# Sixteen buffers for value pages in the residual's place, half of a norm moved into the SSM stage, an operand split in pieces, and the decode product with the cached V turned round

## What is computed

```python
def layer_step(x, lp, sb_fn, s0_re, s0_im, mem_k, mem_v):
    x = half_ffn(x, lp['g_ffn1'], lp['w_ffn1_gate'], lp['w_ffn1_up'], lp['w_ffn1_down'])
    proj = rmsnorm(x, lp['g_mix']) @ lp['w_in']                  # q, k, v, u
    o_sb = sb_fn(q, k, v, lp['sb_bias'])                         # samples: 8192 cached keys each
    o_ssm, s_re, s_im = s5_mix(u, s0_re, s0_im, ...)             # ends in g * sigmoid(g @ w_glu + b_glu)
    mixed = jnp.concatenate([rmsnorm(o_sb, lp['g_sb_out']), rmsnorm(o_ssm, lp['g_ssm_out'])], axis=-1)
    x = x + mixed @ lp['w_out']
    x = x + cross_attend(rmsnorm(x, lp['g_xattn']), lp['w_xq'], lp['w_xo'], mem_k, mem_v)
    x = half_ffn(x, lp['g_ffn2'], lp['w_ffn2_gate'], lp['w_ffn2_up'], lp['w_ffn2_down'])

def memory_kv(mem, g_mem, w_xk, w_xv):
    hm = rmsnorm(mem, g_mem)
    return hm @ w_xk, hm @ w_xv          # the prompt's 256 memory rows

def cross_attend(h, w_xq, w_xo, mem_k, mem_v):
    s = jnp.einsum('blhd,bmhd->bhlm', q, mem_k) * (X_HEAD_DIM ** -0.5)
    o = jnp.einsum('bhlm,bmhd->blhd', jax.nn.softmax(s, axis=-1), mem_v)
```

## Time and profile before

| | us |
|---|---|
| median of 3 runs | 3155.11 (3146.27 to 3157.51) |
| the profiled execution | 3153.33 |
| its span | 3151.7 |
| TensorE busy | 2832.8 (90% of the span) |
| VectorE busy | 1722.9 (55%) |
| ScalarE busy | 905.1 (29%) |
| GpSimd busy | 635.7 (20%) |
| mean granted clock | 0.931 |

### The profile page before, as it was taken

One profiled execution on the slowest core, in us unless ns is written; L12 is line 12 of the kernel. 1 busy time (PEld: TensorE's weight loads), 2 busy tenths in 40 slices (PEclk: granted clock), 3 DMA queues, 4 the chain that ended last, 5 costly groups with the idle time before them and its releaser, 6 DMA issues. The chain is left out here.

```text
span 3151.7 us, 45173 instructions
## 1 busy us (share of the span) xinstructions
PE 2832.8 (90%) x15561; PEld 2272.7 (72%) x15561; DVE 1722.9 (55%) x2217; ACT 905.1 (29%) x1691; POOL 635.7 (20%) x827
## 2 busy tenths in 40 slices
PE   6778899999999899988869679998989999999998
PEld 4456565665666677855514669877989999999997
DVE  7559999988989945247350353544253222222226
ACT  4221111121111123059600441422043233333324
POOL 1010123223223000000122050022002223332223
PEclk8788999999999999999878789997899999999999
DMA  9866799989989711100366231134101111111111
GB/s 357 328 208 190 260 313 338 318 313 316 319 311 348 225 41 54 40 28 28 110 213 216 60 121 47 41 114 163 51 29 53 47 43 44 40 40 53 41 46 54
DMA packets 337781, 469.77 MB, mean 149 GB/s; under 512 B 26422, under 2 KB 215219, under 8 KB 336028
## 3 DMA queue, kind: packets, MB, share of 16 engines
q1 hardware_dynamic: 299748, 341.35, 33.1%
q0 software_dynamic: 37296, 125.54, 11.3%
q10 hardware_dynamic: 552, 0.57, 0.1%
HBM read 448.99 MB, written 18.39 MB: 148 GB/s over the span
## 5 line engine op out<-in xcount | busy, mean ns | idle before, releaser
L83 DVE TENSOR_TENSOR wlo<-raw,whi 128x1024 fp32r<-128x1024 f32 (+1 forms) x182 | 221.6, 1227 | 399.3 <-ACT whi L79 399.3
L106 PE MATMUL banks<-ffn_ghi,whi 128*128 128x344 f32 (+1 forms) x880 | 323.5, 368 | 68.8 <-DVE ffn_glo L1612 37.5
L79 ACT ACTIVATE whi<-raw 128x1024 fp32r<-128x1024 f32 (+1 forms) x192 | 197.5, 1041 | 612.7 <-PE banks L108 477.0
L1823 POOL TENSOR_TENSOR xT<-xT,ffn_down 128x344 f32<-128x344 f32 x264 | 249.2, 946 | 550.6 <-ACT ffn_down L1867 546.5
L106 PE MATMUL banks<-ffn_hhi,whi 128*128 128x344 f32 x1056 | 340.0, 322 | 8.4 <-DVE ffn_hlo L136 5.7
L107 PE MATMUL banks<-ffn_hlo,whi 128*128 128x344 f32 x1056 | 338.8, 321 | 0.0
L108 PE MATMUL banks<-ffn_hhi,wlo 128*128 128x344 f32 x1056 | 338.8, 321 | 0.0
L606 POOL DMA_DIRECT2D ffn_vt<-in_cache_v_dram x384 | 206.1, 537 | 648.9 <-issue 635.2
L619 DVE TENSOR_TENSOR ffn_kt<-ffn_kt,ffn_q 128x1024 f32<-128x1024 f32 x256 | 311.6, 1217 | 39.1 <-DMA ffn_kt<-in_cache_k_dram 38.9
L108 PE MATMUL banks<-ffn_ghi,wlo 128*128 128x344 f32 (+1 forms) x880 | 315.7, 359 | 0.0
L624 DVE TENSOR_REDUCE ffn_z<-ffn_kt 128x16 f32<-128x1024 f32 x256 | 311.7, 1218 | 6.5
(11 more groups left out here) (427 smaller groups left out, 4993.9 us busy)
## 6 DMA issues: line engine op xcount, KB each, us to landing
ffn_kt<-in_cache_k_dram SPq DMA_DIRECT2D x512, 256.0 KB, 4.3
ffn_vt<-in_cache_v_dram POOLq DMA_DIRECT2D x384, 256.0 KB, 5.2
raw<-in_w_ffn_gate_dram SPq DMA_DIRECT2D x44, 512.0 KB, 3.9
raw<-in_w_ffn_up_dram SPq DMA_DIRECT2D x44, 512.0 KB, 4.0
raw<-in_w_ffn_down_dram SPq DMA_DIRECT2D x44, 512.0 KB, 4.6
s_vt<-in_cache_v_dram SPq DMA_DIRECT2D x64, 256.0 KB, 4.3
s_vt<-in_cache_v_dram POOLq DMA_DIRECT2D x64, 256.0 KB, 4.5
a_wide<-in_w_ffn_gate_dram SPq DMA_DIRECT2D x11, 1024.0 KB, 9.8
```

Of the source, the lines that this page charges most:

```text
L79: act.activation(self.k.whi[c % W_RING][:, 0:self.width], self.k.raw[:, c % RAW_RING, 0:self.width], ACT.Copy).then_inc(self.hi_done, 1)
L83: dve.tensor_tensor(self.k.wlo[c % W_RING][:, 0:self.width], self.k.raw[:, c % RAW_RING, 0:self.width], self.k.whi[c % W_RING][:, 0:self.w ...
L106: pe.matmul(out, whi, rhi, start=first, stop=False)
L1823: pool.tensor_tensor(x, x, dt_[:, m % DR, 0:n], ALU.add).then_inc(added, 1)
```

## The change

It has six parts.

1. `Values.VR` is 16, and `s_vt` lies where `xT` lies. `xT` is written to a scratch in DRAM at attention's start (`x_away`) and read back in the SSM stage's SyncE program once all pages are weighed (`x_back`). The first 16 pages are asked for early: eight by SyncE before ck, the taps and the pages' weights, eight by GpSimd before it makes its mask. Two waits on TensorE's progress before the page loop are gone.
2. The norm of oT's prompt columns (`first_half`) is made in the SSM stage: squares on ScalarE after the states, additions, inverse and products on VectorE, sums on TensorE after the second part of y, roots on ScalarE before the third take. ScalarE waits for the twelve products before the turn takes.
3. glu's operand is split in three pieces of 344 columns, and TensorE waits for one piece a tile. The high parts of glu's first weights are made between the takes.
4. In memory the rows are loaded ahead (`rows_ahead`), only ossm and the eight sample columns of oT are normed, and all of that is on ScalarE and VectorE; GpSimd has nothing. The weight ring there has four buffers.
5. In all stages with `Late`, the wlo of units 1 and 2 are VectorE's, placed between the operand's pieces.
6. In cross, weights padded to 32 columns (a sample's four at b, b + 8, b + 16, b + 24) are stationary and V moves, 512 columns at a time, 32 matmuls that all add into PSUM partitions 0 to 31 of two banks. A mask product on VectorE keeps each head's own columns, and 8 matmuls with `sel` sum and turn them. GpSimd makes pad and mask at the stage's start.

```diff
+    def __init__(self, k, name, width=D, more=()):
         self.k, self.width = k, width
+        self.slots = [k.raw[:, r] for r in range(RAW_RING)] + list(more)
+        self.ring = len(self.slots)
...
-    def pool_ahead(self, pool):
-
-        for n in (1, 2):
-            pool.wait_ge(self.w.lo_done, n + RAW_RING)
-            self.w.lo(pool, n, n)
...
         self.w.lo(v, 0, 0)
+        later = {self.late.count() - 4: 1, self.late.count() - 1: 2}
         for m in range(self.late.count()):
             self.late.lo(v, m)
+            if m in later:
+                self.w.lo(v, later[m], later[m])
...
-                if self.late and n == 0:
-                    v.wait_ge(self.w.lo_done, 3 + RAW_RING)
...
+                if self.operand and n == 0:
+                    self.operand(pe, t)
...
-    VR = 8
+    VR = 16
...
+    FIRST_PAGES = range(VR)
+    OTHERS = range(VR, COUNT * 64)
+
     def prepare(self, pool):
+        pool.wait_ge(self.pages_in, 16)
+        pool.wait_ge(self.k.x_away, 16)
+        self.load(pool, 0, self.FIRST_PAGES)
         pool.memset(self.mask[:, :], 1.0).then_inc(self.consts, 1)
...
+        for n in pages[parity::2]:
...
+                sp.dma_start(self.x_dram, self.xT[:, :, :].rearrange("p k n -> p (k n)")).then_inc(self.x_away, 16)
...
+        self.first_half = Late(self, "mn0", [(0, 344), (344, 344), (688, 336)], lambda k, t0, n: self.oT[:, k, t0:t0 + n], None, None,
+                               None, place("s_nsquare", [P, 4, 344], 26.5), place("s_nacc", [P, 3, 344], 16),
+                               place("s_nroot", [P, NT], 60), place("s_nmean", [P, 3, 344], 21.125), [4, 5], blocks=4)
+        self.m_rows = place("m_rows", [P, 2, D], 0)
+        late_v = Values(self, self.nc.alloc_sbuf_tensor_at("s_vt", [P, Values.VR, 512], F32, offset=self.x_offset), place("s_vw", [P, Values.COUNT, 512], 41.25),
...
+                sp.wait_ge(late_v.pages_in, 16)
+                sp.wait_ge(self.x_away, 16)
+                late_v.load(sp, 1, late_v.FIRST_PAGES)
                 for i in range(2):
...
-                sp.wait_ge(late_v.pages_in, 16)
-                sp.wait_ge(q["gm_in"], 32)
-                sp.wait_ge(q["quad"], kinds["final"])
-                late_v.load(sp, 1)
+                late_v.load(sp, 1, late_v.OTHERS)
...
+                sp.wait_ge(late_v.v_used, 16 * Values.COUNT)
+                sp.dma_start(self.xT[:, :, :].rearrange("p k n -> p (k n)"), self.x_dram).then_inc(self.x_back, 16)
+                sp.wait_ge(q["taken"], kinds["turn"] + 9)
+                sp.dma_start(self.m_rows[:, :, :], a["mem_prompt"].rearrange("(b p) n -> p b n", p=P)).then_inc(self.rows_ahead, 16)
...
-                pool.wait_ge(q["quad"], kinds["final"])
-                late_v.load(pool, 0)
+                late_v.load(pool, 0, late_v.OTHERS)
...
+                act.wait_ge(q["v"], self.ssm_states)
+                for t_ in range(3):
+                    self.first_half.squares(act, t_)
                 for i in range(8):
+                    if i == 2:
+                        for t_ in range(3):
+                            self.first_half.roots(act, t_)
...
+                act.wait_ge(q["scaled"], 12)
                 for i in range(8):
+                    if i == 6:
+                        for n in range(2):
+                            glu.w.hi(act, n, n, 1)
...
-                act.activation(ghi[:, :, :], gT[:, :, :], ACT.Copy).then_inc(q["split_hi"], 1)
-                glu.act_ahead(act)
+                for t_, (t0, n) in enumerate(ALL_TILES):
+                    act.activation(ghi[:, :, t0:t0 + n], gT[:, :, t0:t0 + n], ACT.Copy).then_inc(q["split_hi"], 1)
+                    if t_ == 0:
+                        glu.w.hi(act, 2, 2, 2)
...
+                for t_ in range(3):
+                    self.first_half.adds(v, t_)
+                for t_ in range(3):
+                    self.first_half.invert(v, t_)
+                    t0, n = self.first_half.tiles[t_]
+                    for k in range(4):
+                        x = self.oT[:, k, t0:t0 + n]
+                        v.tensor_tensor(x, x, self.first_half.inverse_rms(t_), ALU.mult).then_inc(q["scaled"], 1)
                 for b in range(Values.COUNT):
                     late_v.own_heads(v, b)
-                v.wait_ge(q["split_hi"], 1)
-                v.tensor_tensor(glo[:, :, :], gT[:, :, :], ghi[:, :, :].bitcast(F32), ALU.subtract).then_inc(q["split_lo"], 1)
-                glu.dve_ahead(v)
+                for n in range(2):
+                    glu.w.lo(v, n, n)
+                for t_, (t0, n) in enumerate(ALL_TILES):
+                    v.wait_ge(q["split_hi"], t_ + 1)
+                    v.tensor_tensor(glo[:, :, t0:t0 + n], gT[:, :, t0:t0 + n], ghi[:, :, t0:t0 + n].bitcast(F32),
+                                    ALU.subtract).then_inc(q["split_lo"], 1)
+                    if t_ == 0:
+                        glu.w.lo(v, 2, 2)
...
+                        if kind == "y" and i == 1:
+                            for t_ in range(3):
+                                self.first_half.sums(pe, t_)
...
-                sp.dma_start(rows[:, :, :], a["mem_prompt"].rearrange("(b p) n -> p b n", p=P)).then_inc(rows_in, 16)
...
-            @block.gpsimd
-            def _(pool):
-                def scale(i, t):
-                    half = halves[i]
-                    pool.wait_ge(half.inverse, 3 * t + 3)
-                    for k in range(4):
-                        t0, n = ALL_TILES[t]
-                        x = half.src(k, t0, n)
-                        pool.tensor_tensor(x, x, half.inverse_rms(t), ALU.mult).then_inc(mixed, 1)
-                proj.pool_ahead(pool)
-                for g, (i, t) in enumerate(NORMS):
-                    halves[i].adds(pool, t)
-                    if g >= 3:
-                        scale(*NORMS[g - 3])
-                for i, t in NORMS[3:]:
-                    scale(i, t)
...
+                    if n in (2, 3, 4, 5):
+                        i, t = NORMS[n - 2]
+                        halves[i].adds(v, t)
+                    if n in (7, 8, 9, 10):
+                        i, t = NORMS[n - 7]
+                        half = halves[i]
+                        half.invert(v, t)
+                        t0, size = half.tiles[t]
+                        for k in range(4):
+                            x = half.src(k, t0, size)
+                            v.tensor_tensor(x, x, half.inverse_rms(t), ALU.mult).then_inc(mixed, 1)
...
+                pe.wait_ge(self.rows_ahead, 16)
...
+                pool.memset(pad[:, :, :, :], 0.0).then_inc(q["consts"], 1)
+                pool.memset(mask[:, :], 1.0).then_inc(q["consts"], 1)
...
-                        v.tensor_copy(wT[:, :, :], ps[1][:, 0:64].rearrange("p (k m) -> p k m", k=2)).then_inc(q["w_out"], 1)
+                        v.wait_ge(q["consts"], 4)
+                        for b in range(NS):
+                            v.tensor_copy(pad[:, b, :, b:32:NS], ps[1][:, 0:64].rearrange("p (k h b) -> p k h b", k=2, b=NS)[:, :, :, b]).then_inc(q["padded"], 1)
...
+                v.wait_ge(q["all_v"], 1)
+                v.tensor_tensor(masked[:, :], self.psum[0:32, 1024:2048], mask[:, :], ALU.mult).then_inc(q["kept"], 1)
...
-                pe.wait_ge(q["w_out"], 1)
                 pe.wait_ge(q["exped"], GR)
                 for b in range(NS):
+                    pe.wait_ge(q["padded"], b + 1)
                     pe.wait_ge(cache_in[b % 4], 16 * (2 + b // 4 + 1))
-                    for c in range(KD):
-                        for k in range(2):
-                            m = (c // 2) * NS + b
-                            ins = pe.matmul(ps[2][:, c * NS + b:c * NS + b + 1], cache[:, b % 4, k, c * P:(c + 1) * P],
-                                            wT[:, k, m:m + 1], start=k == 0, stop=k == 1)
-                    ins.then_inc(q["columns"] if b == NS - 1 else q["v_used"], 1)
+                    for k in range(2):
+                        for half in range(2):
+                            ins = pe.matmul(ps[2 + half][0:32, :], pad[:, b, k], cache[:, b % 4, k, half * 512:(half + 1) * 512],
+                                            start=b == 0 and k == 0, stop=b == NS - 1 and k == 1)
+                    ins.then_inc(q["all_v"] if b == NS - 1 else q["v_used"], 1)
+                pe.wait_ge(q["kept"], 2)
+                for k in range(KD):
+                    ins = pe.matmul(ps[4][:, k * NS:(k + 1) * NS], masked[:, k * P:(k + 1) * P], sel[:, :], start=True, stop=True)
+                ins.then_inc(q["columns"], 1)
```

132 lines of the change are left out of this document (64 added, 68 removed).

## The result

The changed kernel takes 3052.55 us (median of 4, 3043.79 to 3055.68), the kernel before on the same chip 3156.31 (median of 4, 3146.27 to 3161.82): a ratio of 0.967, 95% interval 0.9638 to 0.9702. The prediction was 3066 with a range of 3042 to 3100.

A forecast was written before the change was run, and what follows sets the result against it. TensorE was busy 90% of the span, mostly in untouched feed-forward blocks, so weaker stretches counted: 3153.33 − 40 (SSM) − 24 (memory) − 5 (stage starts) − 20 (V product) = 3064.3, as a median 3066; range 3042 to 3100.

The forecast's parts named there:

- a quad: Weighing ahead of y: four value pages, 1 MB, would cost 2.5 us at the DMA's rate, or 4.3 at 242 GB/s.
- present pages: Inside y: two quads weighed with pages already there take 2.1 us, a part 6.4; −1.6 × 6 = −10.
- The two cold parts: First two parts of y, 23 us at clock 0.50, expected to stay because a thinly filled stretch precedes them.
- Rival (a): SSM gains only about 10, through pages at 242 GB/s or y at half clock throughout: 3096; chance 0.19.
- The loading ahead: Memory stage: rows loaded ahead cut TensorE's wait of 7.0 us after glu's last matmul; −4.4, leaving 2.6.
- the way to the first sum: Memory stage: VectorE's m_lo and m_acc run free without GpSimd's work, so 3.74 us before the first sum halves; −3.5.
- The units: Memory's sixteen units: waits for mn_acc and slow clock go, VectorE's new work costs some 3 us; body 53, −16.
- the signs of being wrong: Listed: s_vt waits in y, clock 0.5 beyond two parts, VectorE's wlo ending waits, TensorE waits for toep or page weights.
- (b): Cross stage: the samples' V product runs at half clock, +9 instead of −20: 3095; chance 0.12.
- (c): Cross stage: the V product streams at 0.134 us a record: 3053; counted within the forecast's chance of 0.58.
- (d): Late weight tiles, not pages, open the weighing at 1600; y gains 15 plus 10: 3075, within the forecast's 0.58.
- (e): Slower than before: early pages delay the toep taps on SP's queue, and y cannot start without them; chance 0.05.

The follow-up runs named there:

- v_alone: The kernel before with only the changed cross stage (stationary padded weights, V moving): 3129.67 us, ratio 0.9923.
- ring8: The changed kernel with eight page buffers instead of sixteen, still filled early: 3092.26 us, ratio 0.98.
- gluwhole: The changed kernel with glu's operand split whole again and its weights' halves after it: 3070.38 us (one run).
- v4: The changed kernel with the samples' V product spread over four groups of 32 PSUM partitions instead of one: 3050.97 us, ratio 0.9675.
- vold: The changed kernel with the cross stage of the kernel before: 3075.82 us, ratio 0.9762.

## Why the prediction was right, and where it was not

- **Pages and the start of y.** Forecast 1621 for y's first matmul by the states; it came at 1621.69, with weighing from 1585.54 (forecast 1587) to 1621.76 (forecast 1616). The late weights were right as a mechanism (6.5 us of waiting); a quad cost 3.1 us, not 2.5. Weighing and states end together, so both bound y now; in nine of the ten other traces with sixteen buffers asked for in either way the weighing ends last. Against v_alone (71.1 us from gsum to y) the gain is 17.3, not 23.
- **Inside y.** Forecast −1.6 a part by present pages: parts of 6.1 us, and 64.9 − 51.2 = 13.7 against v_alone, where the sum had 10 and +2.4 for the sums. The step that failed is "The two cold parts (23 us at 0.50) stay as they are: both before and after, a thinly filled stretch precedes them." The low clock was read from one execution, and neither ring8 nor v_alone, whose weighing is as thin from its first matmul on (33.4 of 52.5 us, 36.0 of 56.0, against 38.5 of 60.75), shows it. Rival (a) fell in both its forms: the pages came at 324 GB/s, not 242, and y did not stay at half clock. The three sums took 2.29 us.
- **glu.** Forecast −5, measured −4.6 in the pair and −4.7 against gluwhole.
- **Memory.** −24 was forecast in three terms, −30.4 measured. The loading ahead was right at −4.4. Of the way to the first sum, −5.2 for −3.5, the mechanism named was not the one: the wait for m_acc did not halve but went from 3.74 to 3.23, while the waits for m_hlo fell from 6.3 us in three to 3.6 in one. The units were mis-sized, −20.8 for −16: VectorE's wlo did end a wait, which the prediction lists among the signs of being wrong, but a single one of 1.72 us, at unit 13, where the sum had 3 us; the slow clock around the old waits returned in full: the stretch's clock rose from 0.86 to 0.97.
- **Stage starts.** 5 was forecast for four; mix 1.8 to 2.1, cross_queries 0.9 and project_in about 1 were seen, and in ffn2 nothing can be seen under its spread.
- **V product.** Forecast 0.45 a record and 32.5 up to the last small record, measured 0.43 and 30.9; up to xo's start, 34.7 for 56.3 before, −21.6 for −20. Rivals (b), half clock, and (c), 0.134, both fell: the clock was 1.00, and v4 shows what (c) would have needed.
- **Left out.** The prompt's part of cross, +6.7. The sum took a stage that gains only four short operations on GpSimd, one on VectorE ahead of the scalings and the copies at its end for unchanged; it never asked how near GpSimd's products lie to VectorE's. They are near enough for 0.3 us to decide.
- Rivals (d) and (e): the weights' landing did delay the weighing, by less than (d) had it (first weighing at 1585.54, not 1600), though such a wait stood among the signs of being wrong; TensorE did not wait for the taps at all.

The sum came to −89 and the trace to −97.6. Against the sum, y gave 13.6 more (7.5 of it the clock of one execution; of the rest, some 4.7 the two early parts, whose weighing also shrank, and 1.4 the six later ones) and memory 6.5 more; the collision in cross took 6.7 back, and the two feed-forward blocks with xo another 6.7, which lies within what they vary between the traces. That the misses of either sign nearly cancel, and that the 22.5 us for y's start were met although some 6 of the 23.2 belong to the slow execution before, is luck.

## What to carry to other kernels

A ring of landing buffers is worth what its depth lets the DMA reach: eight pages gave 242 to 258 GB/s and sixteen 324 to 383, while asking earlier gave about 7 us with eight pages and 1 to 3 with sixteen. A stationary operand of 32 columns costs as much as one of 128 until its outputs are spread over the four groups of PSUM partitions. Before pricing a stage at a low clock, look whether another execution of the same code shows it, and before calling a stage untouched, look how close GpSimd's long two-input operations pass VectorE's short ones.

## What the runs showed of the hardware

- A VectorE scaling of 4 elements a partition that starts behind a GpSimd product of 128 × 2048 (4.5 us) ends when that product does, whatever is left of it. Over all groups of the stage and all traces, 37 scalings were held up and took 2.05 to 4.36 us, and 36 of them ended 0.02 to 0.03 us after the end of a product; the other 67 took 0.17.
- The same weighing and y code ran at a granted clock of 0.50 for 23 us in one execution and at 1.00 in another. What decides it stays open: TensorE's busy share from the first weighing to y was 0.63 in the first, 0.64 in the second and in ring8 (which also stayed at 1.00), and 0.78 in vold, where 0.50 came for 6.8 us of y.
- A transfer that waits for a DRAM write of 32 KB was issued 3.1 to 4.5 us after that write in the same place of 14 traces, enough to turn the order above.
